# A two-layer decoder trunk on one core: the attention stage reordered with four score buffers, an added mask and two value banks, and the gated recurrent mixer's gate half reordered with premultiplied scan inputs

## The reference, cut to what matters

```python
def stick_breaking_block(q_blk, q_pos, k, v):          # 8 heads x 64
    z = einsum('bhqd,bhkd->bhqk', q_blk, k) / sqrt(64)
    mask = k_pos[None, :] < q_pos[:, None]
    log_not = where(mask, log_sigmoid(-z), 0.0)
    later = (reverse cumulative sum of log_not over keys, without the own key)
    w = where(mask, exp(log_sigmoid(z) + later), 0.0)
    return einsum('bhqk,bhkd->bhqd', w, v)

# even layer, mixer
    u = conv_a * sigmoid(conv_gate)
    u = causal_depthwise_conv(u, conv_w, conv_b)       # 31 taps, 512 channels
    u = silu(layer_norm(u, conv_ln_g, conv_ln_b))
    h = h + concatenate([u, attention]) @ w_out        # then a SwiGLU, width 2688
# odd layer, mixer
    gate, xb = split(rms_norm(h) @ w_in)               # 1408 channels each
    gate = gelu(gate)
    xb = causal_depthwise_conv(xb)                     # 4 taps
    r, i = sigmoid(block-diagonal gates of xb)
    a = exp(-8 r softplus(-lambda));  bx = sqrt(1 - a*a) * (i * xb)
    h_t = a_t * h_{t-1} + bx_t
    h = h + (gate * h_t) @ w_out                       # then top-2-of-8 experts, width 3584
```

## Time and profile before

| | |
|---|---|
| median of 3 runs | 1396.59 us (1396.23 to 1401.37) |
| the profiled execution, its own time | 1398.92 us |
| its span | 1397.1 us |
| PE busy | 1330.4 us (95%) |
| DVE / ACT / POOL busy | 792.5 (57%) / 642.6 (46%) / 18.1 us (1%) |
| HBM traffic | 424 MB read, 304 GB/s over the span |
| granted TensorE clock, mean | 0.979 |

### The profile page before, as it was taken

One profiled execution on the slowest core, in us unless ns is written; L12 is line 12 of the kernel. 1 busy time (PEld: TensorE's weight loads), 2 busy tenths in 40 slices (PEclk: granted clock), 3 DMA queues, 4 the chain that ended last, 5 costly groups with the idle time before them and its releaser, 6 DMA issues.

```text
span 1397.1 us, 18640 instructions
## 1 busy us (share of the span) xinstructions
PE 1330.4 (95%) x7469; PEld 1007.4 (72%) x7469; DVE 792.5 (57%) x807; ACT 642.6 (46%) x589; POOL 18.1 (1%) x16
## 2 busy tenths in 40 slices
PE   7998899999989699999999999999999999999997
PEld 6977899999989678886346887346888335888433
DVE  5984456665484868993108983106995104987101
ACT  5454544443469366772007873006874004875100
POOL 0002000000002000000000000000000000000000
PEclk9998899999999899999999999999999999999999
DMA  9331355454455279998999999999999999999995
GB/s 329 101 114 31 93 179 171 140 181 159 152 160 169 89 295 386 366 367 323 404 408 409 413 409 409 391 409 410 412 408 411 412 407 412 412 406 413 407 407 233
DMA packets 149573, 426.35 MB, mean 305 GB/s; under 512 B 7664, under 2 KB 65648, under 8 KB 135152
## 3 DMA queue, kind: packets, MB, share of 16 engines
q1 hardware_dynamic: 149488, 425.12, 80.1%
HBM read 424.04 MB, written 1.05 MB: 304 GB/s over the span
## 4 chain that ended last, share of the span: by engine, by line
PE 77%; DMA 7%; DVE 6%; ACT 5%; issue 3%; SPq 2%; DVEq 0%; ACTq 0%
PE P L1592 55%; PE P L1990 12%; DMA over_gates_raw<-in_moe_w_gate 5%; PE P L2014 3%; PE P L1877 2%; SPq L587 2%; DVE raw_lo L1036 1%; DMA raw<-in_moe_w_down 1%; ACT whi L656 1%; PE P L1898 1%; PE P L1932 1%; DVE xc L1293 1%; PE P L1696 1%; ACT whi L890 1%; DMA raw<-in_w_in_even 1%
## 5 line engine op out<-in xcount | busy, mean ns | idle before, releaser
L1592 PE MATMUL P<-hn_hi,whi 128*128 128x272 f32 (+1 forms) x640 | 186.9, 292 | 18.5 <-DVE gg L1317 13.1
L1347 DVE TENSOR_TENSOR raw_lo<-raw,whi 128x2048 fp32r<-128x2048 f32 x84 | 189.3, 2285 | 10.7 <-ACT whi L890 10.0
L1592 PE MATMUL P<-whi,xe_hi 128*128 128x512 f32 x448 | 179.1, 400 | 7.1 <-DVE over_gates_lo L1347 7.1
L890 ACT ACTIVATE whi<-raw 128x2048 fp32r<-128x2048 f32 x84 | 160.9, 1918 | 53.8 <-PE P L1592 33.0
L1036 DVE TENSOR_TENSOR raw_lo<-raw,whi 128x2048 fp32r<-128x2048 f32 (+3 forms) x72 | 150.0, 2105 | 61.8 <-ACT whi L656 61.7
L1592 PE MATMUL P<-hn_hi,raw_lo 128*128 128x272 f32 (+1 forms) x640 | 185.0, 289 | 0.0
L1592 PE MATMUL P<-hn_lo,whi 128*128 128x272 f32 (+1 forms) x640 | 184.7, 289 | 0.0
L1592 PE MATMUL P<-whi,xe_lo 128*128 128x512 f32 x448 | 177.3, 396 | 0.0
L1347 DVE TENSOR_TENSOR over_gates_lo<-over_gates_raw,whi 128x2048 fp32r<-128x2048 f32 x72 | 162.8, 2286 | 19.1 <-ACT whi L890 18.6
L890 ACT ACTIVATE whi<-over_gates_raw 128x2048 fp32r<-128x2048 f32 x72 | 137.5, 1918 | 42.4 <-PE P L1592 17.3
L1592 PEld LDWEIGHTS P<-hn_hi,whi 128*128 128x128 f32 x640 | 121.5, 190 | 20.5 <-DVE gg L1317 13.5
(11 more groups left out here) (290 smaller groups left out, 2089.4 us busy)
## 6 DMA issues: line engine op xcount, KB each, us to landing
raw<-in_moe_w_up SPq DMA_DIRECT2D x64, 1024.0 KB, 15.1
raw<-in_moe_w_gate SPq DMA_DIRECT2D x64, 1024.0 KB, 15.1
over_gates_raw<-in_moe_w_down SPq DMA_DIRECT2D x64, 1024.0 KB, 16.5
over_gates_raw<-in_moe_w_gate SPq DMA_DIRECT2D x48, 1024.0 KB, 18.7
raw<-in_moe_w_down SPq DMA_DIRECT2D x40, 1024.0 KB, 15.5
over_gates_raw<-in_moe_w_up SPq DMA_DIRECT2D x32, 1024.0 KB, 16.4
over_xb_raw<-in_moe_w_up SPq DMA_DIRECT2D x16, 1024.0 KB, 15.2
raw<-in_w_in_even SPq DMA_DIRECT2D x10, 1024.0 KB, 10.5
```

Source lines behind the costliest of these rows:

```text
L890: act.activation(whi[u % HI][:, :], moe_raw[k % MOE_RAW][:, :], ACT.Copy).then_inc(hi_ready, 1)
L1347: dve.tensor_tensor(moe_lo(k), moe_raw[k % MOE_RAW][:, :], whi[u % HI][:, :].bitcast(F32), ALU.subtract).then_inc(lo_ready, 1)
L1592: last = pe.matmul(dst, lhs, rhs, start=start and n == 0, stop=stop and n == 2)
```

## The change

In the attention stage:
- zm has four buffers instead of two, so `masked(p)` waits only for the scores. The mask is added (0 or -1e9) instead of multiplied, by the same instruction. The log term then needs no mask: `softplus` is one DVE instruction that writes back into lx, and ll is gone. After the exponential the hidden weights are zero, so POOL's multiplication is gone, and `values` waits for ACT.
- `values(p)` uses banks 6 and 7 in turn.
- The LayerNorm's Silu becomes x / (1 + exp(-x)): on ACT an Identity with gain and bias and an Exp, on DVE an addition, a reciprocal and a multiplication for each of four 128x272 tiles. The two loads of activation tables around the Silu go.
- The output projection's first unit takes its eight input tiles one by one as they are ready.
- The three engines' lists are written in a new order; seven taps of the convolution go in front of `qk_norm(3)`.

In the odd mixer:
- The gate sigmoids move from u = 60 + j to u = 59 + j on ACT, in front of tanh(j - 1), and their table is loaded ahead of them, at u = 58.
- `gelu_input(g)` moves in front of split_lo(66 + g) on DVE, and ACT's `y_high` in front of the gelu.
- (1 + a) is multiplied into the scan's input ahead of the roots (`scan_input`, 11 instructions at u = 65), so a `scan(m)` has two instructions left. The last two scans are one unit apart.

```diff
@@ constants
-                  ("mask", NS), ("negmask", NS), ("tie", NE * NE), ("erow", NE), ("zero8", NE),
+                  ("hide", NS), ("tie", NE * NE), ("erow", NE), ("zero8", NE),
-    put("mask", mask)
-    put("negmask", -mask)
+    put("hide", HIDE * (mask - 1))
-CONV_EARLY, CONV_PER_UNIT, CONV_PER_PAIR = 8, 10, 6
+CONV_EARLY, CONV_PER_UNIT, CONV_LAST, CONV_PER_PAIR = 8, 10, 7, 4
-SCAN_AT = {..., U_GELU + 3: (9, 10)}
+SCAN_AT = {..., U_GELU + 3: (9,), U_GELU + 4: (10,)}
-        zm = sb("zm", [128, 2, 2, NS])
+        zm = sb("zm", [128, HEADS // 2, 2, NS])
-        ll = sb("ll", [128, 2, 2, NS])
+        def values_bank(p):
+            return 6 + p % 2
@@ gpsimd
-            for p in range(HEADS // 2):
-                pool.wait_ge(wexp_ready, p + 1)
-                pool.tensor_tensor(ww[:, p % 2], ww[:, p % 2], both(cst("mask")), ALU.mult).then_inc(w_ready, 1)
@@ scalar, attention
+                log_part(0)
+                log_part(1)
+                split_hi(U_OUT_E)
+                log_part(2)
+                weights(0)
...
+                log_part(3)
+                weights(1)
+                high(0)
+                for c in range(CT): ... Square of cacc[:, c]
+                split_hi(U_OUT_E + 1)
+                weights(2)
+                high(1)
                 act.wait_ge(var_done, 1)
                 inverse_root(rs[:, 0], P[:, 1, 0:T], CONV_CH, var_root)
                 for c in range(CT):
                     act.wait_ge(ln_scaled, c + 1)
-                    act.activation(uin[:, c], cacc[:, c], ACT.Silu, scale=v("ln_g", c), bias=v("ln_b", c))\
+                    act.activation(uin[:, c], cacc[:, c], ACT.Identity, scale=v("ln_g", c), bias=v("ln_b", c))\
+                        .then_inc(ln_out, 1)
+                for c in range(CT):
+                    act.wait_ge(ln_out, c + 1)
+                    act.activation(scr[:, c], uin[:, c], ACT.Exp, scale=-1.0).then_inc(ln_exp, 1)
+                weights(3)
+                high(2)
@@ vector, attention
+                masked(0)
+                masked(1)
+                conv(CONV_PER_PAIR)
+                softplus(0)
+                conv(CONV_PER_PAIR)
+                softplus(1)
+                masked(2)
+                split_lo(U_OUT_E)
+                log_weights(0)
+                masked(3)
+                conv(CONV_PE * CONV_W)
+                softplus(2)
+                log_weights(1)
+                attn_low(0)
+                centre()
+                softplus(3)
+                log_weights(2)
+                attn_low(1)
+                split_lo(U_OUT_E + 1)
...
+                log_weights(3)
+                for c in range(CT):
+                    dve.wait_ge(ln_exp, c + 1)
+                    step(dve.tensor_scalar(scr[:, c], scr[:, c], 1.0, None, ALU.add))
+                    step(dve.reciprocal(scr[:, c], scr[:, c]))
+                    dve.tensor_tensor(uin[:, c], uin[:, c], scr[:, c], ALU.mult).then_inc(ln_silu, 1)
+                attn_low(2)
...
@@ tensor, attention
             taps(U_DIAG)
+            scores(2)
+            later(0)
+            scores(3)
+            taps(U_DIAG + 1)
+            later(1)
+            values(0)
+            conv_mean()
+            later(2)
+            values(1)
+            conv_variance()
+            later(3)
+            values(2)
+            values(3)
@@ scalar, odd mixer
                 if u == U_BAND + 2:
                     xb_high(len(BAND_UNITS) - 1)
+                    act.preload_act_table_set("sigmoid_and_others")
+                if U_BAND <= u - GATES_AHEAD < U_GELU:
+                    gates(u - GATES_AHEAD - U_BAND)
@@ vector, odd mixer
+                    if u == U_GELU - 1:
+                        for m in range(KL):
+                            scan_input(m)
+            def scan_input(m):
+                dve.wait_ge(xi_ready, m // 2 + 1)
+                dve.wait_ge(decay_ready, m + 1)
+                dve.scalar_tensor_tensor(out=ig[:, m], in0=rg[:, m], scalar=1.0, in1=ig[:, m],
+                                         op0=ALU.add, op1=ALU.mult).then_inc(input_scaled, 1)
             for u in range(U_MOE):
+                if U_GELU <= u - AHEAD < U_OUT_O:
+                    gelu_input(u - AHEAD - U_GELU)
```

More of the change, by code:

```diff
@@ L785, in after @@
                     g = u - U_GELU
+                    if g >= 1:
+                        for m in BAND_UNITS[g - 1]:
+                            y_high(m)
                     if u < U_OUT_O:
@@ L1593, in three, with features @@
                 return last
-            def features(u, x_hi, x_lo, bank, k0=0, start=True, stop=True, cols=slice(0, T), norm=None, sums=None):
+            def features(u, x_hi, x_lo, bank, k0=0, start=True, stop=True, cols=slice(0, T), norm=None, sums=None,
+                         mixed=False):
                 k, w = UNITS[u][2], UNITS[u][3]
@@ L1729, in _ @@
             taps(U_DIAG)
-            for p in range(HEADS // 2 + 1):
-                if p + 2 < HEADS // 2:
-                    scores(p + 2)
-                if p == HEADS // 2 - 1:
-                    conv_mean()
-                if p < HEADS // 2:
-                    later(p)
-                if p == 0:
-                    taps(U_DIAG + 1)
-                if p == HEADS // 2 - 1:
-                    conv_variance()
-                if p >= 1:
-                    values(p - 1)
-            pe.wait_ge(ln_lo, CT)
-            pe.wait_ge(attn_lo, CT)
+            scores(2)
[11 more added lines that the diff above has]
+            values(3)
             for u in range(U_OUT_E, U_FFN1):
```

163 lines of the change are left out of this document (66 added, 97 removed).

## The result

The changed kernel takes 1385.81 us (median of 5, 1383.62 to 1389.35) against 1397.09 us (median of 5) of the kernel before, measured together with it: ratio 0.9919, interval [0.9896, 0.9942]. Two later series of measurements, on the unaltered kernel again, gave 0.9902 [0.9869, 0.9934] and 0.9911 [0.9886, 0.9935]. Predicted were 1385.0 us, in a range of 1377 to 1391. The profiled execution took 1389.35 us, the slowest of its five, with a span of 1387.5 us.

A forecast was written before the change was run, and what follows sets the result against it. PE, busy 95% of the span, was taken to bound the kernel through standstills and low clock in the trunk. Attention 4.5 plus gelu half 7.1 gave 11.6 us off the 1396.6 median: 1385.0 us, range 1377 to 1391.

The forecast's parts named there:

- The order of PE in attention: Attention: PE's new list runs without gaps at full clock, so later(3) ends at 125.7 us, 7.5 us earlier.
- The low clock's return: Rival, attention: two half-clock stretches before 130 us return, losing 5.2 us, 1390.2; 13% together with a late decays.
- The tail: Before attention's output projection: four tiles at 2.91 us, reciprocal 2.03 each; projection starts at 139.6, 4.5 us earlier.
- The restart kept as it was: Attention's output projection: the half-clock stretch behind PE's wait stays as long as before; 3 us each way in the range.
- The gelu half: Odd mixer: DVE's shorter list starts the last gelu unit 7.1 us earlier (8.6 - 0.5 - 1.0).
- `decays` "1.0 us later": Odd mixer, ACT: decays come 1.0 us later than 439.48, with bounds of 1 earlier and 2 later.
- The rest of the list: DVE's list up to gelu_input(3): loses 4.1, 2.3 and 2.2 us, gains a 0.5 us wait; 8.6 - 0.5.
- the wait of 0.5 us for split_hi(66): Gelu half, DVE: the new order adds a wait of 0.5 us to the list.
- Passing on "one for one": Trunk to end: what PE gains before the first expert moves the whole rest, one for one; 11.6 us.
- the sign I had set for this step: Passing on is wrong if the first expert starts 12 us earlier and the end does not.
- The premise that the weight stream sets the pace behind the first expert: Experts: from 652 us the weight stream is at full rate, 399 GB/s, and sets the pace, entered when PE gets there.

The follow-up runs named there:

- order_only: Kernel before with only two orders changed: ACT's y_high ahead of the gelu, DVE's gelu_input ahead of split_lo; 1396.17 us, ratio 0.9975.
- gates_only: Kernel before with only the gates taken out of the decay pass and issued three units behind their band; 1398.92 us, ratio 0.9994.
- warm_mix: Changed kernel with 62 unread unit-matrix matmuls on PE in the wait before attention's output projection; 1392.83 us, ratio 0.9945.
- silu_warm: Changed kernel with ACT's Silu behind weights(3) instead of the reciprocals, plus idle matmuls before the projection's tiles and each looped large expert; 1382.20 us, ratio 0.9868.
- The parts alone: Kernel before with only scan inputs multiplied ahead (1396.29 us), or only y_high and gelu_input moved forward (1396.17 us).
- recip_twice: Changed kernel with each of the four reciprocals made a second time into a scratch tile nothing reads; 1393.95 us, ratio 0.9961.
- six kernels that have at most one half: Kernel before, and it with only the attention half (1395.66 us), only the odd-mixer half (1390.85 us), or one of that half's three parts (1396.29, 1398.92, 1396.17 us).
- silu_late: Changed kernel with ACT's own Silu issued behind weights(3) instead of exponential, addition, reciprocal and multiplication; 1380.53 us, ratio 0.9869.
- warm_experts: Changed kernel with 18 unread unit-matrix matmuls on PE in the wait before each looped large expert; 1386.46 us, ratio 0.9901.

## Why the prediction was right, and where it was not

*The order of PE in attention: right.* No idle mark and full clock from 98 us to the last `later`, which ends near 125.8 (125.7 predicted). The low clock's return, a rival, is in none of the profiles with this order. One argument against it was wrong, though. I had written that each low stretch in the trace follows a gap of 1.8 us or more. One does not; it begins in the router, at 518.8 us, with no idle mark above 0.16 us in front of it (timeline of PE before, then windows):

```profile
515.43 3.92 PE L1859 MATMUL P<-router_g,xnt 128*128 128x8 f32 x32 [0.16 <-ACT xnt L908]
519.20 0.57 PE L1864 MATMUL P<-chosen,con 128*128 128x8 f32 x2
```

```profile
516.00:519.00 3.00, 3.00 (x29) 0.96 1.03 410
519.00:524.00 5.00, 2.64 (x12) 0.50 1.03 410
```

*The tail: mis-sized, 1.0 us too dear.* The exponentials were ready as laid out (DVE starts at 127.38, 127.1 taken). The reciprocal took 1.85 us where the line through the earlier trace rows gave 2.03: from 2 to 272 columns that is (1.85 - 0.166) / 270 = 6.2 ns a column, not 6.9. The addition took 0.30 us where I took 0.42 from L1076 and 0.06 more for the step. Together 2.58 a tile instead of 2.91, 1.3 us over four, of which 0.3 went to the later start. The projection came at 138.61 instead of 139.6.
*The restart kept as it was: 0.5 us too dear.* The half clock lasted 4.9 us behind the start (138.61 to 143.51), and about 5.9 before. The lead at the xn mark is 5.98 us: attention gave 6.0 instead of 4.5. What I had not seen is how this 6.0 divides: in the one profile of the old order at clock 1.00 it takes 53.1 us (order_only) and the new one 50.65, so 2.5 us are the new list and some 3.2 us in the profile of before were its low clock, which four of the five profiles of the old order have.

*The gelu half: 9.07 instead of 7.1.* The step that failed is `decays` "1.0 us later". It came 0.73 us earlier, once the attention lead is taken off (439.48 to 432.77, less 5.98). PE's wait for the first gates fell to 2.31 us, and the third band unit then ran at full clock, where the kernel before had the low level behind its 3.68 us. I had no term for that clock. This is 1.7 of the 2.0 us; gates_only measured it alone, 0.70. The term hangs on the clock: in warm_mix and silu_warm, with the same code here, the third band unit restarted at the lower level, the table load of `decays` came 30.4 and 30.5 us behind the xn mark (28.98 in the changed kernel, 29.71 before), 0.7 to 0.8 us later than before, and n = 5 came 1.4 to 1.6 us later than in the changed kernel. There the "1.0 later" would have been nearly right. The changed kernel's three profiles all have the full clock. The rest of the list was right to 0.2 us: 8.6 less 0.5 predicted, 9.07 - 0.73 = 8.34 measured; the wait of 0.5 us for split_hi(66) is 0.27. The parts alone gave 3.35 and 4.49.

*Passing on "one for one": right for a delay, missed for the change.* recip_twice's 6.85 us reached the end in full, within some 3 us. But of 15.05 us at n = 5 the medians show 11.3, 13.1 and 12.7, and in the profiles the first gather is 14.6 us earlier and the end 9.6. By the sign I had set for this step it was wrong. The premise that the weight stream sets the pace behind the first expert holds: no looped pair takes less than 214.9 us in any profile. What I had put at nothing is PE's clock at the restarts there, with which PE holds the stream up. 0.4 us are lost between n = 5 and the first gather (46.60 us before, 47.02 to 47.13 after). The first two looped pairs take 4.8 us more in the first profile after than in that before, which is nearly all of its 5.0 us. In the mean of three profiles after against the six kernels that have at most one half it is 1.8 us. That leaves 15.05 - 0.4 - 1.8 = 12.8 us at the end, within the scatter of the three medians. Why the large experts of those two pairs should restart at half clock more often after (5 of 6, and 5 of 12 in the six kernels) stays open; it may be chance.

So the total was right partly by luck, through two errors of opposite sign: 3.4 us too little in the trunk (1.5 and 2.0), and 2 to 4 us of passing on not foreseen.

## What to carry to other kernels

Look for the instruction that ends a wait before replacing it by cheaper-looking ones on another engine: a table load of 1.28 us was removed here at the price of four reciprocals of 1.85 us each on the path, and moving the load behind the last urgent activation beats both. Cut the trace at a few marks and compare stretches, not the whole: distances in the trunk repeated within some 0.2 us in the changed kernel's three profiles, where the totals of one kernel scattered by 6 us. A wait of PE costs its length and then the clock behind it; behind the short waits here (1.8 to 2.4 us) the second part came in some executions only. What that clock costs the end depends on the stage: where the weight stream had room to catch up, as in the last pair of experts, it cost nothing. Before filling a wait with idle work, count in the trace how many records, and how much time, one of its instructions takes.

## What the runs showed of the hardware

The reciprocal on DVE runs at 6.2 ns a column at 128x272 float32 (1.85 us), against 1.1 to 1.6 for the additions and multiplications beside it. An addition of a constant took 0.30 us where L1076, which multiplies by one operand from a vector and adds another, took 0.417 for the same shape, and a product of two tiles 0.44.

After a wait of 1.7 to 2.4 us PE's clock was at its lower level in some profiles and at 1.00 in others of the same code:

| PE's wait | where | lower level behind it |
|---|---|---|
| 1.74 us | output projection, silu_late | 1 of 1 profile |
| 1.84 to 1.86 us | first log term, old order | 4 of 5 |
| 2.30 to 2.31 us | third band unit, new gates | 2 of 10 |
| 2.07 to 2.40 us | looped large experts, changed kernel | 7 of 9 |
| 1.94 to 2.39 us | the same, kernels with at most one half | 7 of 18 |
| 3.68 us | third band unit, old gates | 4 of 4 |
| 4.96 us | output projection, old order | 5 of 5 |
| 5.6 to 10.6 us | gelu unit n = 5 | 14 of 14 |
| 6.8 to 13.6 us | output projection, new order with the reciprocals | 6 of 6 |

The length of a wait does not decide it alone: 1.84 us brought the lower level more often than 2.31 us did, and at 518.8 us in the kernel before it came with no idle mark above 0.16 us in front. With PE kept busy in the wait the clock was 1.00 in all eight places where this was tried (three starts of large experts in warm_experts and in silu_warm, the projection in warm_mix and in silu_warm).

A looped pair of experts, 88 MB of weights, took no less than 214.9 us in any of the 14 profiles, which is 410 GB/s.

A matmul of a float32 unit matrix with itself is recorded as two, of 0.114 us each.
